# Stick-breaking cumulative sums and GLA scores as products of rounded parts, decay products in two pieces, MLA gate products at other tiles

## The reference, cut to what matters

```python
# stick-breaking attention: 8 heads of 128, two query blocks of 128
z = einsum('bqhd,bkhd->bhqk', qb, k) * scale
sp = where(visible, softplus(z), 0)
tail = cumsum(sp, axis=3, reverse=True) - sp
a = where(visible, exp(log_sigmoid(z) - tail), 0)
# GLA: 4 heads, 256 wide keys, chunks of 64 rows
gk = gk_low @ w_gk2 + b_gk                  # rank 16
log_a = log_sigmoid(gk) / 16
b = cumsum(log_a over the chunk)
q_e = q * exp(b);  k_e = k * exp(-b);  k_last = k * exp(b_last - b)
A = einsum('bhncd,bhnsd->bhncs', q_e, k_e)  # and the state carried from chunk to chunk
# MLA
return (o * silu(gate)) @ w_out
```

## Time and profile before

| | |
|---|---|
| median of 3 runs | 2455.3 us (2453.84 to 2455.58) |
| profiled execution | 2455.41 us |
| its span, first to last instruction | 2453.7 us |
| busy: PE / DVE / ACT / POOL | 2431.6 / 1485.2 / 1242.8 / 32.2 us |
| mean granted TensorE clock | 0.998 of full speed |

### The profile page before, as it was taken

The page is one execution under the profiler, slowest core; times in us unless marked ns, Lnnn a source line. Parts: engine busy times, 40 slices in busy tenths (PEclk is TensorE's granted clock), DMA queues, the critical chain, the costliest instruction groups (busy, mean ns, idle before and its releaser), DMA issues.

```text
span 2453.7 us, 34037 instructions
## 1 busy us (share of the span) xinstructions
PE 2431.6 (99%) x12328; PEld 2064.2 (84%) x12328; DVE 1485.2 (61%) x1820; ACT 1242.8 (51%) x1598; POOL 32.2 (1%) x59
## 2 busy tenths in 40 slices
PE   8999999999999999999999999999999999999998
PEld 6888888888888888888888888888878788799987
DVE  5654544556695565777567765776545455665565
ACT  6554344554445444555445544555454544556553
POOL 2000000000000000000000000000000000000000
PEclk9999999999999999999999999999999999999999
DMA  8664666556566655666666666666655566564554
GB/s 264 185 187 152 205 189 189 158 183 191 158 190 183 210 187 183 186 188 191 195 191 187 192 193 189 191 185 191 182 155 163 176 188 195 156 174 138 155 178 157
DMA packets 421146, 448.33 MB, mean 183 GB/s; under 512 B 29798, under 2 KB 283866, under 8 KB 420515
## 3 DMA queue, kind: packets, MB, share of 16 engines
q1 hardware_dynamic: 419058, 440.80, 59.9%
q0 software_dynamic: 1936, 5.91, 0.9%
q10 hardware_dynamic: 32, 0.01, 0.0%
HBM read 444.55 MB, written 2.10 MB: 182 GB/s over the span
## 4 chain that ended last, share of the span: by engine, by line
PE 97%; ACT 1%; DVE 1%; DMA 1%; issue 0%; SPq 0%; DVEq 0%; ACTq 0%
PE blk L643 91%; PE pa L897 1%; DMA weight_raw<-in_w_mem_kv_dram 1%; PE pa L704 1%; PE pa L681 0%; PE pa L1016 0%; PE pa L695 0%; PE pa L706 0%; PE pa L794 0%; PE pa L776 0%; PE pa L713 0%; PE pa L847 0%; DVE arena L1760 0%; ACT weight L1173 0%; PE pa L992 0%
## 5 line engine op out<-in xcount | busy, mean ns | idle before, releaser
L1760 DVE TENSOR_TENSOR weight<-weight_raw,weight 128x1024 fp32r<-128x1024 f32 (+1 forms) x834 | 1005.6, 1212 | 740.5 <-ACT weight L1173 736.6
L1173 ACT ACTIVATE weight<-weight_raw 128x1024 fp32r<-128x1024 f32 (+1 forms) x834 | 868.6, 1047 | 700.4 <-PE blk L643 652.7
L643 PE MATMUL blk<-weight,h 128*128 128x512 f32 (+1 forms) x4632 | 1043.2, 386 | 0.0
L643 PEld LDWEIGHTS blk<-weight,h 128*128 128x128 f32 x4632 | 856.6, 188 | 171.8 <-issue 0.3
L643 PE MATMUL blk<-u,weight 128*128 128x512 f32 x3808 | 667.8, 336 | 1.4 <-DVE weight L1760 1.4
L643 PEld LDWEIGHTS blk<-u,weight 128*128 128x128 f32 x3808 | 577.9, 187 | 86.3 <-DVE weight L1760 1.8
L643 PE MATMUL blk<-weight,u 128*128 128x512 f32 x1920 | 447.0, 393 | 0.3 <-DVE u L1814 0.3
L643 PEld LDWEIGHTS blk<-weight,u 128*128 128x128 f32 x1920 | 360.5, 189 | 76.9 <-issue 2.4
L643 PE MATMUL blk<-h,weight 128*128 128x256 f32 (+1 forms) x896 | 136.0, 313 | 0.0
L643 PEld LDWEIGHTS blk<-h,weight 128*128 128x128 f32 x896 | 124.2, 189 | 11.3
L1760 DVE TENSOR_TENSOR arena<-arena,blk 128x512 f32<-128x512 f32 (+2 forms) x69 | 46.9, 679 | 47.5 <-ACT arena L1546 26.5
(11 more groups left out here) (252 smaller groups left out, 953.4 us busy)
## 6 DMA issues: line engine op xcount, KB each, us to landing
weight_raw<-in_w_in_dram SPq DMA_DIRECT2D x208, 512.0 KB, 3.7
weight_raw<-in_w_up_dram SPq DMA_DIRECT2D x344, 256.0 KB, 3.2
weight_raw<-in_l_gla_w_in_dram SPq DMA_DIRECT2D x96, 512.0 KB, 4.1
weight_raw<-in_w_down_dram SPq DMA_DIRECT2D x84, 512.0 KB, 4.6
weight_raw<-in_l_mla_w_in_dram SPq DMA_DIRECT2D x49, 512.0 KB, 4.0
weight_raw<-in_w_branch_dram SPq DMA_DIRECT2D x48, 512.0 KB, 4.7
weight_raw<-in_w_mem_kv_dram SPq DMA_DIRECT2D x32, 512.0 KB, 5.2
weight_raw<-in_w_out_dram SPq DMA_DIRECT2D x32, 512.0 KB, 4.5
```

Source lines behind the costliest of these rows:

```text
L643: mm = nc.tensor.matmul(to, lhsT, rhs, start=(kt == 0 and m == 0), stop=(kt == ph.bt - 1 and m == len(ops) - 1))
L1173: nc.scalar.activation(hi, raw, ACT.Copy).then_inc(hi_made, 1)
L1760: return nc.vector.tensor_tensor(out_, a, b, op)
```

## The change

1. **Stick-breaking.** After POOL's selects, ACT rounds `sb_sp` to `sb_sp_hi` (fp32r, 1536 columns, s = 5) and DVE makes `sb_sp_lo` (s = 6). They lie in free chunks of `u`. In the first set ACT also copies `tri_ge` and `ones` to fp32r. The cumulative sums (now s = 7) are fp32r products, each done for the high and for the low part. A set now takes 15 tiles.
2. **GLA scores.** `g_q` and `g_ke` get high and low parts in `h`: ACT at j = 12 (all of `g_q`), 17, 22, 25, 28 (128, 128, 256, 256 columns of each of the 8 chunks of `g_ke`), DVE at j = 13, 19, 22, 25, 28. Each f32 score product becomes three fp32r products.
3. **Decay products.** Two at j = 1 and two at j = 2 instead of four at j = 1. Most later steps of `side_decay` stand one tile later.
4. **MLA.** In `mlagate1`, `round_gated` moves from j = 7, 9, 12 to 4, 5, 13 and `gated_rest` from 8, 10, 13 to 5, 6, 14. In both gate phases `gate_quarter` moves from 10 to 12.

```diff
@@ TensorE, side_sb
-                if s == 6:
-                    pe.wait_ge(SB["spm"], 2 * (g + 1))
+                if s == 7:
+                    pe.wait_ge(SB["splo"], g + 1)
                     pe.wait_ge(SB["zs"], g + 1)
                     for h in range(4):
-                        nc.tensor.matmul(pa[:, h, 0:S], tri_ge, sb_sp[:, h, 0:S], start=True, stop=False)
-                        nc.tensor.matmul(pa[:, h, P:S], ones[:], sb_sp[:, h, S:TRI], start=False, stop=True)
-                        mm = nc.tensor.matmul(pa[:, h, S:TRI], tri_ge, sb_sp[:, h, S:TRI],
-                                              start=True, stop=True)
+                        for k, part in enumerate((sb_sp_hi, sb_sp_lo)):
+                            nc.tensor.matmul(pa[:, h, 0:S], upto, part[:, h, 0:S], start=(k == 0), stop=False)
+                            nc.tensor.matmul(pa[:, h, P:S], all_, part[:, h, S:TRI], start=False, stop=(k == 1))
+                        for k, part in enumerate((sb_sp_hi, sb_sp_lo)):
+                            mm = nc.tensor.matmul(pa[:, h, S:TRI], upto, part[:, h, S:TRI], start=(k == 0), stop=(k == 1))
@@ TensorE, side_decay
-                if j in (19, 22, 25, 28):
-                    n = (j - 19) // 3
-                    if n == 0:
-                        pe.wait_ge(GL["kl"], 1)
-                    else:
-                        pe.wait_ge(GL["step"], n)
+                if j in (20, 23, 26, 29):
+                    n = (j - 20) // 3
+                    pe.wait_ge(GL["parts_lo"], n + 2)
...
-                            for c in range(2):
-                                mm = nc.tensor.matmul(pa[:, h, at:at + CH],
-                                                      g_ke[:, 2 * h + c, t * P:(t + 1) * P],
-                                                      g_q[:, 2 * h + c, n * CH:(n + 1) * CH],
-                                                      start=(c == 0), stop=(c == 1))
+                            terms = [(ke[:, 2 * h + c, t * P:(t + 1) * P], q[:, 2 * h + c, n * CH:(n + 1) * CH])
+                                     for c in range(2) for ke, q in ((g_ke_hi, g_q_hi), (g_ke_hi, g_q_lo), (g_ke_lo, g_q_hi))]
+                            for m, (ke, q) in enumerate(terms):
+                                mm = nc.tensor.matmul(pa[:, h, at:at + CH], ke, q, start=(m == 0), stop=(m == len(terms) - 1))
@@ ScalarE
+                if s == 5:
+                    act.wait_ge(SB["spm"], 2 * (g + 1))
+                    if g == 0:
+                        nc.scalar.activation(upto, tri_ge, ACT.Copy)
+                        nc.scalar.activation(all_, ones[:], ACT.Copy)
+                    nc.scalar.activation(sb_sp_hi, sb_sp, ACT.Copy).then_inc(SB["sphi"], 1)
...
+                if j == 12:
+                    act.wait_ge(GL["q"], 1)
+                    nc.scalar.activation(g_q_hi, g_q, ACT.Copy).then_inc(GL["parts_hi"], 1)
+                if j in (17, 22, 25, 28):
+                    n = {17: 0, 22: 1, 25: 2, 28: 3}[j]
...
+                    v = slice(0, (n // 2 + 1) * P)
+                    nc.scalar.activation(g_ke_hi[:, :, v], g_ke[:, :, v], ACT.Copy).then_inc(GL["parts_hi"], 1)
...
-                    if r == 1 and j in (7, 9, 12):
-                        round_gated({7: 0, 9: 1, 12: 2}[j])
+                    if r == 1 and j in (4, 5, 13):
+                        round_gated({4: 0, 5: 1, 13: 2}[j])
@@ VectorE
+                if s == 6:
+                    dve.wait_ge(SB["sphi"], g + 1)
+                    tt(sb_sp_lo, sb_sp, sb_sp_hi.bitcast(F32), ALU.subtract).then_inc(SB["splo"], 1)
...
+                if j == 13:
+                    dve.wait_ge(GL["parts_hi"], 1)
+                    tt(g_q_lo, g_q, g_q_hi.bitcast(F32), ALU.subtract).then_inc(GL["parts_lo"], 1)
+                if j in (19, 22, 25, 28):
+                    n = (j - 19) // 3
+                    if n == 0:
+                        dve.wait_ge(GL["kl"], 1)
+                    dve.wait_ge(GL["parts_hi"], n + 2)
+                    v = slice(0, (n // 2 + 1) * P)
+                    tt(g_ke_lo[:, :, v], g_ke[:, :, v], g_ke_hi[:, :, v].bitcast(F32),
+                       ALU.subtract).then_inc(GL["parts_lo"], 1)
...
-                    if j == 10:
+                    if j == 12:
                         gate_quarter(2 * r)
-                    if r == 1 and j in (8, 10, 13):
-                        gated_rest({8: 0, 10: 1, 13: 2}[j])
+                    if r == 1 and j in (5, 6, 14):
+                        gated_rest({5: 0, 6: 1, 14: 2}[j])
```

More of the change, by code:

```diff
@@ L343, in build_program @@
         sb_z, sb_l, sb_sp = (area(T + n * 4 * TRI, 4, TRI) for n in range(3))
+        sb_sp_hi, sb_sp_lo = (u[:, k, 8:14, :].rearrange("p c s -> p (c s)").rearrange("p (h n) -> p h n", h=4)
+                              for k in range(2))
+        upto, all_ = u_hi[:, 14, 0:P], u_hi[:, 14, P:2 * P]
         index = area(T, NT, INDEX_W)
@@ L363, in build_program @@
         g_e = area(14336, 2 * GH, S)
+        g_q_hi, g_q_lo, g_ke_hi, g_ke_lo = h_hi[:, 0:8], h_lo[:, 0:8], h_hi[:, 8:16], h_lo[:, 8:16]
         g_a = area(14336, 4, TRI)
@@ L468, in build_program @@
                                           "am", "o", "oout", "sq", "inv", "rstd", "on", "turned",
-                                          "hi", "ready", "bias_row", "gain")}
+                                          "hi", "ready", "bias_row", "gain", "parts_hi", "parts_lo")}
         ML = {x: sem(f"mla_{x}") for x in ("k_rows", "zeros", "k_roped", "kturned", "kT", "q_roped", "qturned", "qT",
@@ L985, in side_decay @@
             def side_decay(j):
-                if j == 1:
+                if j in (1, 2):
+                    t = j - 1
                     norm_at(pe, "pre0", "rstd", 2)
@@ L989, in side_decay @@
                     pe.wait_ge(decay_in, 48)
-                    for t in range(NT):
-                        for c in range(2):
-                            mm = nc.tensor.matmul(pa[:, 2 * t + c, :], lowT[0:2 * DECAY_RANK + 1, t * P:(t + 1) * P],
-                                                  w_decay[0:2 * DECAY_RANK + 1, c * 512:(c + 1) * 512],
-                                                  start=True, stop=True)
+                    for c in range(2):
+                        mm = nc.tensor.matmul(pa[:, 2 * t + c, :], lowT[0:2 * DECAY_RANK + 1, t * P:(t + 1) * P],
+                                              w_decay[0:2 * DECAY_RANK + 1, c * 512:(c + 1) * 512],
+                                              start=True, stop=True)
                     mm.then_inc(GL["gk"], 1)
-                if j == 8:
+                if j == 9:
                     pe.wait_ge(GL["la"], 1)
@@ L1381, in side_sb @@
             def side_sb(j):
-                g, s = (0, j) if j < 13 else (1, j - 13)
-                if j >= 26:
+                g, s = (0, j) if j < 15 else (1, j - 15)
+                if j >= 30:
                     return
@@ L1568, in side_decay @@
             def side_decay(j):
[L1569 to L1570 removed]
+                if j == 3:
+                    act.wait_ge(GL["gk"], NT)
                     link(nc.scalar.activation(g_la.rearrange("p t (b c) -> p (t b) c", b=2), allpa, ACT.Abs))
[L1572 removed]
+                if j == 4:
                     link(nc.scalar.activation(g_la, g_la, ACT.Exp, scale=-1.0))
[L1574 removed]
+                if j == 5:
                     nc.scalar.activation(g_la, g_la, ACT.Ln, bias=1.0).then_inc(GL["l"], 1)
[L1576 removed]
+                if j == 10:
                     act.wait_ge(GL["last"], 1)
                     nc.scalar.activation(in_banks(g_e), allpa, ACT.Exp).then_inc(GL["eb"], 1)
[L1579 removed]
+                if j == 13:
                     act.wait_ge(GL["q"], 1)
                     nc.scalar.activation(in_banks(g_e), allpa, ACT.Exp, scale=-1.0).then_inc(GL["enb"], 1)
[L1582 removed]
+                if j == 16:
                     act.wait_ge(GL["diff"], 2 * GH)
@@ L1586, in side_decay @@
                     nc.scalar.activation(small[:, 128:160], small[:, 96:128], ACT.Exp).then_inc(GL["el"], 1)
-                if j == 29:
+                if j == 12:
[4 more added lines that the diff above has]
+                    if n == 0:
+                        act.wait_ge(GL["ke"], 1)
+                    else:
+                        act.wait_ge(GL["step"], n)
+                    v = slice(0, (n // 2 + 1) * P)
+                    nc.scalar.activation(g_ke_hi[:, :, v], g_ke[:, :, v], ACT.Copy).then_inc(GL["parts_hi"], 1)
+                if j == 30:
                     act.wait_ge(GL["rows"], 4)
@@ L2262, in side_decay @@
             def side_decay(j):
-                if j == 5:
+                if j == 6:
                     dve.wait_ge(GL["l"], 1)
```

40 lines of the change are left out of this document (17 added, 23 removed).

## The result

The changed kernel takes 2483.39 us (median of 4 runs, 2480.89 to 2485.64) against 2455.44 us: ratio 1.0115, interval 1.0101 to 1.0128. It is slower by 28 us in the median, 12 more than predicted, and lies outside the range. The profiled execution took 2480.89 us, 25.5 more than that of before (2455.41), and this difference is what the traces are compared over. The four runs lie at two levels, 2481 and 2485.5; the experiments show where the second comes from.

The account below looks back on a forecast made before the run. PE bounds the kernel, busy 2431.6 of 2453.7 us. Score products 5.6 + waits 6.8 + clock 3.2 - cumulative sums 1.4 + their waits 2.5 - MLA 0.7 = +16.0 on 2455.4: 2471 us, range 2461 to 2477.

Parts of the forecast that it names:

- Score products: GLA scores in `glav`: 144 fp32r products at 0.11 us each replace 96 f32 matmuls, +5.6 us.
- (b): Rival, chance 0.1: weight load is no floor for fp32r, narrow products go by their columns; 2456.5 us, no measurable change.
- (c): Rival, chance 0.1: fp32r under 256 columns streams at f32's rate, cumulative sums cost +2.0 us; 2471.6 us.
- (a): Rival, chance 0.2: the clock falls less; 2468 us, or 2466.6 if nothing brings it down.
- (d): Rival, chance 0.15: ACT and DVE chains are shorter, waits halve and one clock fall goes; 2465 us.
- the upper bound of the cumulative sums: Stick-breaking sums for both sets, if 128 columns take f32's 0.21 us: +2.0 us, against -1.4 expected.
- Waits at the scores: GLA scores: PE waits 3.6, 1.6 and 1.6 us for operand parts before groups 1, 3, 4; together +6.8 us.
- Three falls of 1.6 are +4.8: Score stage in `glav`: PE drops to half clock at three score groups, 1.6 us each, +4.8 us.
- The decay products: In `glav`: dealt out in pieces of two, the clock fall behind them goes, -1.6 us.
- Stick-breaking waits: Cumulative sums: PE waits for the new parts, 1.8 us in the first set and 0.7 in the second, +2.5 us.
- The clock: Prediction's paragraph on half clock in `glav`: -1.6 behind decay products, +4.8 at the scores, balance +3.2 us.
- MLA: -0.7 forecast: `mlagate1`: the 1.45 us wait at tile 14 goes, a 0.7 us wait for the copy out of PSUM comes; -0.7 us.

Follow-up runs that it names:

- the part alone: The kernel before with only the stick-breaking part of the change, sums at tile 7 of a set: 2461.64 us, ratio 1.0024.

## Why the prediction was wrong

- **Direction and mechanism: right.** PE bounds the kernel, and the parts of the operands cost it more products and more waits.
- **Score products: right.** 0.11 us was taken, 0.112 measured, also at twice the columns. By the 81 ns that the Trainium skill (TensorE: Matmul & The Clock Gate, "Back-to-back issue gap") gives for pairs of load and matmul at 128 columns, the groups would have taken 11.7 us at full clock and not 15.7; the trace differs for these 4-byte operands. The f32 matmuls of the earlier trace rows stand as far apart inside their groups, 0.112 us: the 0.107 of the prediction is a group's time shared out. From row to row 48 products take 5.27 us, which makes the term 5.3 and not 5.6.
- **Rivals (b) and (c): ruled out.** (b) needs 64 columns in 0.04 us, (c) 128 columns in 0.21 us. At full clock both took 0.11 us, at the scores and in the cumulative sums. As for (a) and (d), the clock fell for longer and not for less, and the waits did not halve. Two side figures of the prediction are off by little and change nothing: 512 columns at 0.229 us exceed 512/2.4 by 16 ns and not 11, and the upper bound of the cumulative sums comes to +1.8 or +1.9 and not +2.0.
- **Waits at the scores: right.** 3.6, 1.6 and 1.6 forecast, 3.34, 1.61 and 1.61 measured. From the end of the cumulative sum to the parts it was 33.5 us, against 33.6 counted.
- **"Three falls of 1.6 are +4.8": the step that failed.** The places were right and the price was not. I carried 1.6 us over from two falls of 3.4 us, one behind the decay products with dense products after it, one behind 3.6 us of idle time with 16 f32 matmuls of 128 columns after it. Here the clock stays at half to the end of the group, each product takes 0.213 instead of 0.112 us, and it returns only some way into the dense products behind: 6.8, 10.2 and 10.2 us at half clock, 13.4 us of time. That is 8.6 of the 9.5 us by which the measured sum (25.5) exceeds the forecast one (16.0). The new products are at most part of the reason: with the old f32 ones behind the same waits the falls were 6.8 us each, already twice what I took. Why a fall lasts 3.4, 6.8 or 10.2 us stays open. The Trainium skill (TensorE: Matmul & The Clock Gate, "HAM oscillation — how this bites in real kernels") puts the penalty at half of the time at half clock; by that 27.3 us would be 13.7, and the trace agrees within 0.3 us. The rule was at hand; the length of the falls was what I had mis-sized.
- **The decay products: right in kind.** The fall went; -1.2 for -1.6. The 84 weight products gained 1.5 us, the two pieces took 0.1 more and the tile between them 0.2.
- **Stick-breaking waits: the first right (1.71 for 1.8), the second not (1.77 for 0.7).** I had POOL faster in the second set. It takes 3.12 us in both. From its end to the parts it is 5.9 us in the first set and 5.5 in the second, without the constants, but PE also comes 0.5 us sooner after it. What I left out altogether is the clock behind these waits: "The clock" speaks of three places in `glav` alone. It costs nothing in some executions and about 5 us in others, which fits the upper two of the four runs, 4.5 us above the profiled one.
- **MLA: -0.7 forecast, -1.9 measured.** The wait of 1.45 went. The new one, for the first copy out of PSUM, is there, 0.5 us from row to row for 0.7. A gain was missed: in the second half of `mlagate1` the copy stood behind `round_gated`. Timeline of ACT and PE before and after:

```profile
2352.16 1.05 ACT L1707 ACTIVATE h<-arena 128x1024 fp32r<-128x1024 f32 x1
2353.11 1.99 ACT L1173 ACTIVATE weight<-weight_raw 128x1024 fp32r<-128x1024 f32 x2
2355.01 1.43 ACT L1359 ACTIVATE arena<-pa 128x1536 f32<-128x1536 f32 x1
```

```profile
2356.49 0.70 PE L704 MATMUL pa<-arena 128*128 128x256 f32 x2 [0.29 <-ACT arena L1359]
```

```profile
2382.05 0.59 PE L708 MATMUL pa<-arena 128*128 128x256 f32 x2
```

In the last row, of the changed kernel, the product with v follows without a wait; in this stretch PE gained 0.6 us.

- **Left open.** Why the fall at the end of the GLA part, behind 3.6 us of idle in every kernel, is 3.4 us long in some profiles and 6.8 in others, no run tells. The same goes for the fall at the first wait of the scores: 6.8 us in the changed kernel's profile, beginning 1.3 us after PE resumed, and 10.2 in four others, beginning between 1.2 us before and 0.2 us after. That the second level of run times is the clock behind the stick-breaking waits rests on profiles of one execution each and on the one level of the kernel without these waits. A version of the scores without any of the three waits was not tried; the products alone cost 5.3 us more than the f32 ones, so no gain is to be expected from it.

## What to carry to other kernels

Where a chain of small steps is made longer, move its reader by as many tiles as it grew: here one tile more made the same stick-breaking change some 7 to 8 us faster. Where columns are few, count loads: a 64-column product in three rounded ones costs three loads, as f32 two, each some 0.11 us. And a wait of PE is not priced at its own length: look at what follows it, and where that is a group of thin products, allow for the whole group at half clock and some of the dense products behind it (here 3.4 to 3.8 us of them, 10.2 us at half clock in all, behind a wait of 1.6).

## What the runs showed that was not expected

- A wait of 1.6 to 1.8 us is enough to bring TensorE to 1.2 GHz. It did so in `glav` in every profile that had the wait, also ahead of the old f32 products, and in stick-breaking in four profiles of six (as from 461.1 to 467.8 us in that of the part alone). The wait of 1.45 us in `mlagate1` before, with weight products on both sides, left it at full. Whether its length or its neighbours made the difference, no run tells.
- Thin products bring the clock down without any idle time: groups of 48 with 64 columns, 0.112 us apart, did, while PE counted as busy throughout, and the same groups with 128 columns did not, in one profile of each.
- Behind a wait the groups of 48 ran at half clock for all but their first 1.8 to 2.7 us, with 64 columns and with 128, in each of the three profiles that have them; without the wait they took 5.3 to 6.0 us instead of 7.9 to 8.6.
